# Two norms from one pass over x, and the sums of three norms set between the tiles of a projection, in a fused two-block kernel

## The chip, the cores and the metric

The kernel runs on one core of a Trainium2 chip. The metric is the time that the device takes for one run, in microseconds (us), as the median of several runs; the lower it is, the better. The core has a matrix engine (TensorE, PE in the rows, with its weight loads as PEld), a vector engine (VectorE, DVE), an engine for activation functions (ScalarE, ACT), a general engine (GpSimd, POOL), and queues that issue DMAs (SyncE's, SP, and GpSimd's). Each engine executes its instructions in the order written; they wait for each other at semaphores.

## The reference, cut to what matters

512 tokens of width 1024 go through a first block (a state-space mixer, a gated FFN with a short convolution, shared keys and values, stick-breaking attention, a second FFN), and through a second one (softmax attention over 256 context tokens and the 512 tokens, then a Hyena layer). What the change touches:

```python
# end of the first block
x = x + conv_ffn(rms_norm(x, norm_ffn[1]), ...)
x = rms_norm(x, norm_final)
# second block, i = 0: softmax attention over context and tokens
h_lat = rms_norm_2(x, norm_w[0]) * (1 + scale) + shift
h_ctx = rms_norm_2(ctx, norm_w[0]) * (1 + scale_c) + shift_c
x = x + gate * attention(h_lat, h_ctx) @ w_out
# i = 1: Hyena
h = rms_norm_2(x, norm_w[1]) * (1 + scale) + shift
x = x + gate * hyena(h) @ w_out
return rms_norm_2(x, final_norm_w)
```

with rms_norm(x, g) = x / sqrt(mean(x^2) + eps) * g, in fp32.

## The kernel before, in words

Activations lie with the width on the partitions: x is eight tiles (k = 0 to 7) of 128 x 512. Large projections run as three matmuls in a 22-bit format instead of one in fp32: weights and inputs are split into a high and a low part. A weight tile of 128 output columns arrives in panels (`raw`, four buffers); ScalarE makes the high part of a panel (`split_hi`, line 1231), GpSimd the low one (`split_lo`, line 1677), and TensorE multiplies hi*hi, lo*hi and hi*lo. The parts have two buffers: `split_hi(n)` waits until TensorE has read panel n - 2. `lin_split` takes one panel for a tile (so `split_hi` of tile t + 2 waits for tile t), the FFN's second projection (`down`) three panels for a tile. After each tile VectorE adds it to x (`add_x`), which raises `x_ready`. `beside(m)` names work that a projection puts behind tile m, `mid(t)` work in the middle of tile t.

A wide norm goes like this: ScalarE squares the eight k tiles (`row` or `norm`), into four buffers, so that square k + 4 waits for the sum of k (`sq_used`). TensorE sums each over the partitions with four matmuls of 32 columns against ones (`sums`, or `norm` at line 508). ScalarE takes the root (line 1210), VectorE the reciprocal (line 1825), TensorE spreads it over all partitions (`spread`, line 527), and VectorE scales (`norm`, lines 1840 and 1843) and adds the shift (lines 1846 and 1849). `keep_clock(n)` puts n matmuls of the unit matrix, 256 columns, in TensorE's order (line 469).

The order of each engine is written out by hand. In the first FFN the norm `kv` already has its squares and sums beside the tiles of `down0`. Behind `down1` the order of TensorE is: norm "final" (sums, spread), norm "nw0" of its result (sums, spread), sums of the context, then "qa" (line 544) from the modulated tokens, with the context's spread behind qa's second tile; then keys and values of both, from one buffer HA that holds context and tokens. The context comes by a DMA in GpSimd's queue, issued when all of down1's tiles are done (line 1750). The norm "nw1" stands behind "wo2", the projection of the softmax attention (its sums before the Hyena filters, line 1052, its spread between them), and "final2" behind "wo3", at the end of the kernel. In wo2 two small matmuls of the filters' hidden layer stand behind tiles 1 and 4 (`hidden`, line 1026).

Of the kernel before, what the change touches and what calls it, by code (L numbers as in the profile page):

```python
# [27 lines left out]
P = 128  # L28
D = 1024
# [41 lines left out]
def build(nc, A, out):  # L71
    ctx = ExitStack()
    with ctx:
# [38 lines left out]
        def col(n, i=0, r=P):  # L112
# [13 lines left out]
            "rn_ready",  # L126
# [316 lines left out]
        R_RELEASE = {"final": ("h_ready", 16), "nw0": ("h_ready", 24), "ctx": ("h_ready", 32),  # L443
                     "final2": ("out_done", 8)}
        WIDE_NORMS = ("mix0", "ffn0", "kv", "ffn1", "final", "nw0", "ctx", "nw1", "final2")

        def sq_of(name, k):

            return bigv(P1 + k * L, L) if name in ("mix0", "ffn0", "ffn1") else sq[:, (k % 4) * L:(k % 4 + 1) * L]

        def rows_of(name):

            i, n = WIDE_NORMS.index(name), norm_src(name)[1]
            return rms[0:n // 4, (i % 2) * P:(i % 2 + 1) * P]
# [5 lines left out]
        def _(pe):  # L460
# [10 lines left out]
            def sums(name, ks):  # L471

                o = take(pe, ("norm", name)) if ks[0] == 0 else ps(("norm", name))
                for k in ks:
# [6 lines left out]
                    if name == "kv" and k < KT - 1:  # L481
                        i.then_inc(S["sq_used"], 1)
# [15 lines left out]
            def norm(name):  # L498

                src, n, m, _ = norm_src(name)  # L500
                keep_clock(3 if name == "nw0" else 0)
                o = take(pe, ("norm", name))
                for k in range(len(src)):
# [9 lines left out]
                    if k < len(src) - 1:  # L513
                        i.then_inc(S["sq_used"], 1)
                fills(i, ("norm", name))
                if name in WIDE_NORMS and name not in ("mix0", "ctx", "nw1"):
                    spread(name)
# [190 lines left out]
            def ffn(l):  # L708
# [6 lines left out]
                for m in range(KT):  # L715
# [20 lines left out]
                    if l == 0 and m == 4:  # L736
                        sums("kv", range(4))
# [122 lines left out]
            norm("final")  # L860


            norm("nw0")
            norm("ctx")
            nh[0] += 8
            lat = lambda k: HA[:, k, LC:LA]
            lin("qa", A["in_q"], 2, lat, wait=h_wait, beside=lambda m: spread("ctx") if m == 1 else None)
            enter_halves([full(("down1", 7))])
            nh[0] += 8
            pe.wait_ge(S["h_ready"], nh[0] + 8)  # L870
            nh[0] += 8
            s, wp = panel(pe, A["in_kv"][0][:, :], KT)
            for seg, (a, b) in enumerate(((0, LC), (LC, LA))):
                key = ("ka", seg)
                o = take(pe, key)
                for k in range(KT):
                    i = pe.matmul(o[:, 0:b - a], wp[:, k, 0:P], HA[:, k, a:b], start=k == 0, stop=k == KT - 1)
                fills(i, key)
            for t2 in range(2):
                key = ("va", t2)  # L880
                o = take(pe, key)
                for t_ in range(3):
                    for k in range(KT):
                        t0 = (3 * t2 + t_) * P
                        i = pe.matmul(o[:, t_ * P:(t_ + 1) * P], HA[:, k, t0:t0 + P], wp[:, k, P:2 * P],
# [8 lines left out]
            for seg, (a, b) in enumerate(((0, LC), (LC, LA))):  # L894
                for what, c0, c1, r0 in (("ckv", 0, P, 0), ("kpe", P, 160, 64)):
                    key = (what, seg)
                    o = take(pe, key)
                    for k in range(KT):
                        i = pe.matmul(o[r0:r0 + c1 - c0, 0:b - a], wp[:, k, c0:c1], HA[:, k, a:b], start=k == 0,
# [119 lines left out]
            def hidden(m):  # L1019
                if m not in HID_BESIDE:  # L1020
# [6 lines left out]

            enter_halves([full(("s", 39))])
            lin_split(lambda t: ("wo2", t), A["attn_w_out"], 8, lambda k: pe.wait_ge(S["g_hi"], k + 1),
                      lambda k: pe.wait_ge(S["g_lo"], k + 1), beside=hidden, x_base=32, h=H_PARTS["wo2"])  # L1030
# [3 lines left out]
            norm("nw1")  # L1034
# [86 lines left out]
            def convolve(t):  # L1121
# [11 lines left out]
                if t in BACK_AT:  # L1133
# [8 lines left out]
                      lambda k: pe.wait_ge(S["z_lo"], k + 1), x_base=40, h=H_PARTS["wo3"])  # L1142
            norm("final2")
# [31 lines left out]
        def _(act):  # L1175
# [38 lines left out]
            eps = small[:, 639:640]  # L1214

# [26 lines left out]
            def row(name, k):  # L1242
                x_wait(k)
                gained(name, k)
                if name == "kv" and k >= 4:
                    act.wait_ge(S["sq_used"], n_used[0] + k - 3)
                act.activation(sq_of(name, k), X[:, k, :], ACT.Square).then_inc(S["sq_ready"], 1)

            def root(name):
                act.preload_act_table_set("sqrt_and_others")  # L1250
                act.wait_ge(*full(("norm", name)))
                frees(act.activation(rows_of(name), ps(("norm", name))[:, 0:P], ACT.Sqrt, bias=eps, scale=1.0 / D),
                      ("norm", name))
                n_x[0] += 8
                n_used[0] += 7 * (name == "kv")
# [84 lines left out]
            def ffn(l):  # L1340
# [1375 lines left out]
```

## Time and profile before

| what | value |
|---|---|
| time, median of 3 runs | 2172.17 us (2170.03 to 2172.68) |
| profiled execution: span from its first to its last instruction | 2169.1 us |
| its own time, beside the span | not given apart; the median lies 3.07 us over the span |
| TensorE busy | 2086.0 us (96%) |
| VectorE busy | 1365.7 us (63%) |
| ScalarE busy | 815.8 us (38%) |
| GpSimd busy | 774.9 us (36%) |
| DMA | 201.85 MB moved, 93 GB/s on the mean |

The profile comes from one execution. Where an engine is busy nearly all the time, what counts is where it stands still and what it is made to execute; of the others, only the pieces that lie between two pieces of TensorE.

### The profile page before, as it was taken

The numbers are of one execution on the slowest core, as the hardware profiler recorded it, in microseconds if no ns is written. First come the engines' busy times: TensorE is split into PE (matmuls) and PEld (weight loads), VectorE is DVE, ScalarE is ACT, GpSimd is POOL, SyncE is SP. The second block draws the span as 40 slices with busy tenths as digits, with TensorE's granted clock in tenths as the row PEclk, the third lists the DMA queues.
The fourth block names the chain that finished last, engine by engine and source line by source line (L and its number), as shares of the span: only waits on it lengthen the run. The fifth ranks groups of instructions, "written<-read, shape, count | busy, mean of one in ns | idle before, by whom it ended". The sixth has DMA issues, their size and how long they took to land.

```text
span 2169.1 us, 28247 instructions
## 1 busy us (share of the span) xinstructions
PE 2086.0 (96%) x11100; PEld 1608.4 (74%) x11100; DVE 1365.7 (63%) x2342; ACT 815.8 (38%) x1185; POOL 774.9 (36%) x462
## 2 busy tenths in 40 slices
PE   7949999999999999999999999999999999999998
PEld 6847778888878877788888875564877646777786
DVE  8563399995656478578884124257776674477752
ACT  3414333333234378333333132244664342322222
POOL 6614456555445521344444430122000322321232
PEclk9979999999999999999999999998999999999999
DMA  5032344443335421244443331012001313222221
GB/s 189 2 45 88 97 137 145 146 136 110 118 123 136 121 57 28 70 135 146 145 140 96 94 128 71 29 47 63 2 15 38 125 78 131 90 80 78 107 72 65
DMA packets 57892, 201.85 MB, mean 93 GB/s; under 512 B 10521, under 2 KB 11721, under 8 KB 54207
## 3 DMA queue, kind: packets, MB, share of 16 engines
q1 hardware_dynamic: 40464, 156.92, 22.7%
q0 software_dynamic: 13568, 41.94, 6.3%
q10 hardware_dynamic: 3728, 1.18, 0.3%
q8 instruction: 89, 1.46, 0.3%
q14 instruction: 43, 0.35, 0.1%
HBM read 179.04 MB, written 10.49 MB: 87 GB/s over the span
## 4 chain that ended last, share of the span: by engine, by line
PE 86%; DVE 8%; ACT 3%; issue 1%; POOL 1%; DMA 1%; SPq 0%; DVEq 0%; ACTq 0%; POOLq 0%
PE psum L675 15%; PE psum L682 15%; PE psum L676 15%; PE psum L725 3%; PE psum L726 3%; PE psum L727 3%; PE psum L1114 3%; PE psum L1072 3%; PE psum L1099 2%; PE psum L1000 2%; PE psum L978 2%; PE psum L968 2%; PE psum L564 2%; PE psum L544 1%; PE psum L1052 1%
## 5 line engine op out<-in xcount | busy, mean ns | idle before, releaser
L1677 POOL TENSOR_TENSOR w_lo<-raw,w_hi 128x1024 fp32r<-128x1024 f32 (+1 forms) x224 | 562.1, 2510 | 826.5 <-ACT w_hi L1231 826.3
L1231 ACT ACTIVATE w_hi<-raw 128x1024 fp32r<-128x1024 f32 (+1 forms) x224 | 233.9, 1045 | 835.8 <-PE psum L682 643.5
L675 PE MATMUL psum<-h_hi,w_hi 128*128 128x512 f32 x800 | 319.1, 399 | 1.6 <-ACT h_hi L1325 1.0
L676 PE MATMUL psum<-h_hi,w_lo 128*128 128x512 f32 x800 | 311.7, 390 | 0.0
L682 PE MATMUL psum<-h_lo,w_hi 128*128 128x512 f32 x800 | 198.0, 389 | 0.0
L675 PE MATMUL psum<-f_lo,w_hi 128*128 128x512 f32 x480 | 189.6, 395 | 2.3 <-POOL w_lo L1677 2.2
L676 PE MATMUL psum<-f_lo,w_lo 128*128 128x512 f32 x480 | 187.3, 390 | 0.0
L675 PEld LDWEIGHTS psum<-h_hi,w_hi 128*128 128x128 f32 x800 | 150.3, 188 | 38.5 <-ACT h_hi L1325 3.3
L676 PEld LDWEIGHTS psum<-h_hi,w_lo 128*128 128x128 f32 x800 | 150.3, 188 | 32.1 <-issue 2.2
L682 PEld LDWEIGHTS psum<-h_lo,w_hi 128*128 128x128 f32 x800 | 150.0, 188 | 31.3 <-issue 0.2
L1221 ACT ACTIVATE big<-psum 128x384 f32<-128x384 f32 (+6 forms) x182 | 90.0, 533 | 165.0 <-PE psum L978 47.6
L725 PE MATMUL psum<-f_hi,w_hi 128*128 128x512 f32 x352 | 138.0, 392 | 0.4
L726 PE MATMUL psum<-f_hi,w_lo 128*128 128x512 f32 x352 | 137.2, 390 | 0.0
L682 PE MATMUL psum<-f_lo,w_hi 128*128 128x512 f32 x496 | 124.1, 390 | 0.0
L682 PEld LDWEIGHTS psum<-f_lo,w_hi 128*128 128x128 f32 x496 | 92.8, 188 | 19.5 <-issue 0.4
L675 PEld LDWEIGHTS psum<-f_lo,w_hi 128*128 128x128 f32 x480 | 90.1, 188 | 22.6 <-issue 2.4
L676 PEld LDWEIGHTS psum<-f_lo,w_lo 128*128 128x128 f32 x480 | 90.2, 188 | 18.2
L2144 DVE SCALAR_TENSOR_TENSOR ffn_buf<-scr,cols,ffn_buf 128x511 f32<-128x511 f32 x44 | 71.8, 1632 | 43.5 <-ACT ffn_buf L1360 43.4
L727 PE MATMUL psum<-f_lo,w_hi 128*128 128x512 f32 x224 | 87.2, 389 | 0.0
L725 PEld LDWEIGHTS psum<-f_hi,w_hi 128*128 128x128 f32 x352 | 66.1, 188 | 15.9 <-POOL w_lo L1677 1.6
L726 PEld LDWEIGHTS psum<-f_hi,w_lo 128*128 128x128 f32 x352 | 66.1, 188 | 13.2
L1828 DVE RECIPROCAL rms<-rms 128x512 f32<-128x512 f32 (+1 forms) x9 | 27.0, 2998 | 74.6 <-ACT rms L1210 74.6
(439 smaller groups left out, 4133.4 us busy)
## 6 DMA issues: line engine op xcount, KB each, us to landing
raw<-in_ffn_w_up SPq DMA_DIRECT2D x88, 512.0 KB, 3.6
raw<-in_ffn_w_down SPq DMA_DIRECT2D x32, 512.0 KB, 3.5
raw<-in_hy_in SPq DMA_DIRECT2D x32, 512.0 KB, 5.7
ffn_buf<-in_ada_w POOLq DMA_DIRECT2D x28, 512.0 KB, 5.1
sq<-in_ada_w POOLq DMA_DIRECT2D x20, 512.0 KB, 5.0
raw<-in_ssm_w_glu SPq DMA_DIRECT2D x16, 512.0 KB, 3.6
spec<-big SPq DMA_DIRECT2D x8, 1024.0 KB, 3.8
big<-spec SPq DMA_DIRECT2D x8, 1024.0 KB, 4.9
```

The costliest lines, as they stand in the source:

```text
L675: pe.matmul(o, hi[:, k, :], h_of(k), start=k == 0, stop=False)
L676: pe.matmul(o, lo[:, k, :], h_of(k), start=False, stop=False)
L682: i = pe.matmul(o, hi[:, k, :], l_of(k), start=False, stop=k == KT - 1)
L725: pe.matmul(o, hi[:, k, :], FHI[:, kk, :], start=kk == 0, stop=False)
L726: pe.matmul(o, lo[:, k, :], FHI[:, kk, :], start=False, stop=False)
L727: i = pe.matmul(o, hi[:, k, :], flo(l, kk), start=False, stop=kk == FT - 1)
L1072: i = pe.matmul(o, tab[:, 2 * par + t, f * P:(f + 1) * P], FE[u % 2][:, a // 2, 2 * par + t, :], start=t == 0, stop=t == 1)
L1114: i = pe.matmul(o[:, par * 256:par * 256 + 256], YW[:, f, 2 * q + par, c * P:(c + 1) * P], tab[:, f, par * 256:par * 256 + 256], start=f = ...
L1221: frees(act.activation(dst, ps(key) if src is None else src, func, **kw), key)
L1231: act.activation(w_parts(n)[0], raw[:, (n % 4) * HALF:(n % 4) * HALF + w], ACT.Copy).then_inc(S["w_hi"], 1)
L1677: pool.tensor_tensor(lo, raw[:, (n % 4) * HALF:(n % 4) * HALF + w], hi.bitcast(F32), ALU.subtract) \
L2144: step(STT(g[:, 1:L], z[:, 0:L - 1], col(f"conv{l}", FT + m), g[:, 1:L], ALU.mult, ALU.add))
```

## The change

Six edits, in three places.

1. The norms "final" and "nw0". With r the inverse root mean square of x, the norm of the final norm's result is r * x * w over the root of mean((r x w)^2) + eps; with both sides multiplied by 1 / r, the second root is taken of mean(w^2 x^2) + eps * (mean(x^2) + eps), that is of mean((w^2 + eps) x^2) + eps^2. So both norms need one pass over x: ScalarE squares each k twice, once as it is and once scaled by the root of w^2 + eps (a column, `sum_weight`), and TensorE sums both into two halves of one bank. This happens beside the tiles of down1, one k per tile, as in down0; the modulated tokens are scaled from x itself before x is normed. "final" is spread behind qa's second tile.
2. The context's squares, sums, root, spread and scaling move into down1 (behind its tiles 1 to 4), in place in XC; its DMA is issued in down1. Keys and values read the context from XC instead of HA (`tokens`).
3. The tokens' shift goes from VectorE to ScalarE (`Identity` with a bias column).
4. The square-root table is loaded at the start of down1, and no longer between the norms; for nw1 and final2 the load goes from before the squares to behind them (`root`).
5. The squares and sums of "nw1" stand beside wo2's tiles and those of "final2" beside wo3's: ScalarE squares row t - 1 behind `split_hi` of panel t + 2; TensorE sums rows 0 to 3 behind tile 4 and row m - 1 behind tile m from 5 on.
6. `keep_clock` before a spread has six matmuls instead of three, for nw0 and final2; the three before nw0's sums go.

```diff
+        SPACED = ("kv", "nw0", "nw1", "final2")
...
+                    if name == "nw0":
+                        for j in range(4):
+                            i = pe.matmul(o[32 * j:32 * j + 32, P:2 * P], mat("ones")[:, 0:32],
+                                          weighted_sq(k)[:, j * P:(j + 1) * P], start=False, stop=k == KT - 1,
+                                          skip_group_check=True)
...
-                keep_clock(3 if name in ("final", "nw0", "final2") else 0)
+                keep_clock(6 if name in ("nw0", "final2") else 0)
...
-                    if l == 0 and m == 4:
-                        sums("kv", range(4))
+                    if m == 4:
+                        sums("nw0" if l else "kv", range(4))
+                    if l:
+                        if m == 2:
+                            norm("ctx")
+                        if m == 3:
+                            spread("ctx")
+                        if m >= 5:
+                            sums("nw0", (m - 1,))
...
-            norm("final")
-            norm("nw0")
-            norm("ctx")
+            sums("nw0", (KT - 1,))
+            spread("nw0")
...
-            lin("qa", A["in_q"], 2, lat, wait=h_wait, beside=lambda m: spread("ctx") if m == 1 else None)
+            lin("qa", A["in_q"], 2, lat, wait=h_wait, beside=lambda m: spread("final") if m == 1 else None)
...
+            def beside_wo2(m):
+                hidden(m)
+                if m == 4:
+                    sums("nw1", range(4))
+                if m >= 5:
+                    sums("nw1", (m - 1,))
...
-            norm("nw1")
+            sums("nw1", (KT - 1,))
...
-                      lambda k: pe.wait_ge(S["z_lo"], k + 1), x_base=40, h=H_PARTS["wo3"])
-            norm("final2")
+                      lambda k: pe.wait_ge(S["z_lo"], k + 1), x_base=40, h=H_PARTS["wo3"],
+                      beside=lambda m: sums("final2", range(4) if m == 4 else (m - 1,)) if m >= 4 else None)
+            sums("final2", (KT - 1,))
+            spread("final2")
... ScalarE: the squares, the root, the end of down1's gates
+                if name in SPACED and k >= 4:
                     act.wait_ge(S["sq_used"], n_used[0] + k - 3)
-                act.activation(sq_of(name, k), X[:, k, :], ACT.Square).then_inc(S["sq_ready"], 1)
+                i = act.activation(sq_of(name, k), X[:, k, :], ACT.Square)
+                if name == "nw0":
+                    i = act.activation(weighted_sq(k), X[:, k, :], ACT.Square, scale=sum_weight(k))
+                i.then_inc(S["sq_ready"], 1)
...
             def root(name):
-                act.preload_act_table_set("sqrt_and_others")
+                if name != "nw0":
+                    act.preload_act_table_set("sqrt_and_others")
...
                 gate_hi(FT - 1)
+                if l:
+                    act.preload_act_table_set("sqrt_and_others")
                 for n in range(n0 + 2 * FT + 2, n0 + HALVES):
                     split_hi(n)
                     m = (n - n0 - 2 * FT) // 3
-                    if l == 0 and (n - n0 - 2 * FT) % 3 == 2 and m:
-                        row("kv", m - 1)
+                    if (n - n0 - 2 * FT) % 3 == 2 and m:
+                        if l and m == 1:
+                            context_squares()
+                            ...
+                        row("nw0" if l else "kv", m - 1)
+                        if l and m == 3:
+                            context_root()
... ScalarE: wo2 (wo3 alike, with "final2")
                 split_hi(HALVES_AT["wo2"] + t + 2)
                 if t == 3:
                     hidden(0)
+                if t:
+                    row("nw1", t - 1)
             hidden(1)
             act.wait_ge(S["hid_ready"], 2)
-            norm("nw1", ready=x_wait)
+            for k in range(5, KT):
+                row("nw1", k)
+            root("nw1")
... GpSimd
+                if n == 2 * FT + 2:
+                    pool.wait_ge(*full(("up1", 2 * FT - 1)))
+                    pool.dma_start(XC[:, :, :], A["ctx"][:, :, :]).then_inc(S["ctx_in"], 16)
... VectorE
-            norm("final", lambda k: col("final", k), lambda k: X[:, k, :])
-            norm("nw0", ...)
-            norm("ctx", ...)
+            dve.wait_ge(*full(("rb", "nw0")))
+            for k in range(KT):
+                STT(HA[:, k, LC:LA], X[:, k, :], adac(0, 1, k), ps(("rb", "nw0")), ALU.mult, ALU.mult) \
+                    .then_inc(S["lat_scaled"], 1)
+            ...
+            dve.wait_ge(*full(("rb", "final")))
+            for k in range(KT):
+                STT(X[:, k, :], X[:, k, :], col("final", k), ps(("rb", "final")), ALU.mult, ALU.mult) \
+                    .then_inc(S["x_normed"], 1)
```

## Rows read from the trace of the kernel before

**Rows 1.** The page: busy time of each engine, share of the span, instructions.
```profile
PE 2086.0 (96%) x11100; PEld 1608.4 (74%) x11100; DVE 1365.7 (63%) x2342; ACT 815.8 (38%) x1185; POOL 774.9 (36%) x462
```

**Rows 2.** The chain of waits, 1286 to 1334: start us, length us, what.
```profile
1286.52 0.84 PE psum L508 x24
...
1304.51 14.88 PE psum L544 x32
...
1320.02 13.93 PE psum L544 x32
```

**Rows 3.** The timeline of the gap: start us, length us, engine, line, operation, count [idle before].
```profile
1287.28 0.69 DVE L2031 TENSOR_TENSOR X<-scr,X 128x512 f32<-128x512 f32 x1
...
1289.24 0.16 PEld L508 LDWEIGHTS psum<-sq,mats 128*32 128x32 f32 x8 [0.36 <-ACT sq L1198]
...
1291.24 1.13 PE L527 MATMUL psum<-rms,mats 128*128 128x128 f32 x8
...
1292.41 5.36 DVE L1840 SCALAR_TENSOR_TENSOR X<-X,cols,psum 128x512 f32<-128x512 f32 x8 [1.31 <-PE psum L527]
1293.25 5.18 ACT L1198 ACTIVATE sq<-X 128x512 f32<-128x512 f32 x8 [1.84 <-DVE X L1840]
...
1294.02 0.93 PE L508 MATMUL psum<-sq,mats 128*32 128x128 f32 x16 [0.36 <-ACT sq L1198]
```

**Rows 4.** The timeline of wo2, tile 6's start, and of its end.
```profile
1707.71 0.39 PE L675 MATMUL psum<-h_hi,f_hi 128*128 128x512 f32 x1
...
1707.97 1.06 ACT L1231 ACTIVATE f_hi<-raw 128x1024 fp32r<-128x1024 f32 x1 [5.62 <-PE psum L682]
...
1718.79 0.75 DVE L2035 SCALAR_TENSOR_TENSOR X<-psum,ada,X 128x512 f32<-128x512 f32 x1 [3.60 <-PE psum L682]
1719.23 2.19 ACT L1198 ACTIVATE sq<-X 128x512 f32<-128x512 f32 x4 [6.17 <-PE psum L508]
...
1721.84 0.70 PE L1052 MATMUL psum<-big 65*128 65x512 f32 x1
```

**Rows 5.** The timeline of the end of wo3.
```profile
2154.82 0.75 DVE L2035 SCALAR_TENSOR_TENSOR X<-psum,ada,X 128x512 f32<-128x512 f32 x1 [4.69 <-PE psum L682]
...
2158.00 0.37 ACT L1210 ACTIVATE rms<-psum,small 128x128 f32<-128x128 f32 x1 [0.55 <-PE psum L508]
...
2159.50 1.13 PE L527 MATMUL psum<-rms,mats 128*128 128x128 f32 x8
```

**Rows 6.** ScalarE's timeline at both ends of down1; TensorE's waits, 1160 to 1290.
```profile
1174.42 0.83 ACT L1231 ACTIVATE w_hi<-raw 128x768 fp32r<-128x768 f32 x1
...
1277.96 1.28 ACT L1190 ACT_TABLE_LOAD   x1
1279.26 2.19 ACT L1198 ACTIVATE sq<-X 128x512 f32<-128x512 f32 x4
...
PEld psum L725 <- POOL w_lo L1677: 0.5, 1, 0.5
```

**Rows 7.** TensorE's timeline: one group of sums in ffn1, four in down0.
```profile
925.73 0.39 PE L676 MATMUL psum<-h_hi,w_lo 128*128 128x512 f32 x1
926.04 0.42 PE L478 MATMUL psum<-big,mats 128*32 128x128 f32 x8
926.40 2.12 PE L682 MATMUL psum<-h_lo,w_hi 128*128 128x512 f32 x8
...
585.31 1.08 PE L478 MATMUL psum<-sq,mats 128*32 128x128 f32 x32
```

**Rows 8.** ScalarE's timeline and groups of context squares; the context's DMA (KB, us to landing).
```profile
1192.62 1.06 ACT L1231 ACTIVATE w_hi<-raw 128x1024 fp32r<-128x1024 f32 x1 [4.59 <-PE psum L727]
...
L1198 ACT ACTIVATE sq<-Hb 128x256 f32<-128x256 f32 x8 | 2.7, 405 | 0.5 <-PE psum L508 0.5
...
Hb<-in_ctx POOLq DMA_DIRECT2D x1, 1024.0 KB, 5.2
```

**Rows 9.** Busy time by window: us, PE, PEld, DVE, ACT, POOL, granted clock, DMA share, GB/s.
```profile
1297.00:1301.00 4.00, 3.76 (x29) 2.20 (x30) 1.72 (x3) 3.14 (x6) 0.00 (x0) 0.57 0.01 2
```

More of the change, by code:

```diff
@@ L876, in _ @@
                 for k in range(KT):
-                    i = pe.matmul(o[:, 0:b - a], wp[:, k, 0:P], HA[:, k, a:b], start=k == 0, stop=k == KT - 1)
+                    i = pe.matmul(o[:, 0:b - a], wp[:, k, 0:P], tokens(k, a, b), start=k == 0, stop=k == KT - 1)
                 fills(i, key)
@@ L1214, in _ @@
             eps = small[:, 639:640]
+            eps_squared = small[:, 638:639]
             def x_wait(k):
@@ L1441, in _ @@
             ffn(1)
-            norm("final", ready=x_wait)
-            n_x[0] += 8
-            norm("nw0", ready=lambda k: act.wait_ge(S["h_ready"], 8 + k + 1))
-            act.wait_ge(S["ctx_in"], 16)
-            norm("ctx")
+            row("nw0", 7)
+            root("nw0")
+            for k in range(KT):
+                act.wait_ge(S["lat_scaled"], k + 1)
+                act.activation(HA[:, k, LC:LA], HA[:, k, LC:LA], ACT.Identity, bias=ada[:, 2 * k:2 * k + 1]) \
+                    .then_inc(S["h_ready"], 1)
             def lat_parts(ks):
                 for k in ks:
-                    act.wait_ge(S["h_ready"], 16 + k + 1)
+                    act.wait_ge(S["h_ready"], 8 + k + 1)
                     act.activation(LAT_HI[k], HA[:, k, LC:LA], ACT.Copy).then_inc(S["lat_hi"], 1)
@@ L1618, in _ @@
                 split_hi(HALVES_AT["wo3"] + t + 2)
-            norm("final2", ready=x_wait)
+                if t:
+                    row("final2", t - 1)
+            for k in range(5, KT):
+                row("final2", k)
+            root("final2")
         @block.gpsimd
@@ L1745, in _ @@
                     ada_load(ADA_ISSUE[1][n])
+                if n == 2 * FT + 2:
+                    pool.wait_ge(*full(("up1", 2 * FT - 1)))
+                    pool.dma_start(XC[:, :, :], A["ctx"][:, :, :]).then_inc(S["ctx_in"], 16)
             pool.wait_ge(S["x_ready"], 32)
-            for m in range(8):
-                pool.wait_ge(*full(("down1", m)))
-            pool.dma_start(XC[:, :, :], A["ctx"][:, :, :]).then_inc(S["ctx_in"], 16)
+            pool.wait_ge(*full(("norm", "nw0")))
             pool.dma_start(ROPE[:, :, :], A["rope"][:, :, :]).then_inc(S["rope_in"], 16)
@@ L2089, in ada_finish @@
                     own()
+                fv = cols[:, COLS["final"]:COLS["final"] + 8]
+                weights_ = ada[:, 49:65:2]
+                step(TT(ada[:, 16:32:2], ada[:, 16:32:2], fv, ALU.mult))
+                step(TT(weights_, fv, fv, ALU.mult))
+                own()
+                step(TS(weights_, weights_, EPS, None, ALU.add))
+                own()
             def norm_split(name, gain, shift, ks, r):
@@ L2166, in finish @@
                         ada_finish()
+                    if m == 3:
+                        dve.wait_ge(*free(("norm", "ctx")))
+                        dve.reciprocal(rows_of("ctx"), rows_of("ctx")).then_inc(S["rn_ready"], 1)
+                    if m == 4:
+                        dve.wait_ge(*full(("rb", "ctx")))
+                        for k in range(KT):
+                            step(STT(XC[:, k, :], XC[:, k, :], adac(0, 1, k, 1), ps(("rb", "ctx"))[:, 0:LC], ALU.mult,
+                                     ALU.mult))
+                            own()
+                            TS(XC[:, k, :], XC[:, k, :], adac(0, 0, k, 1), None, ALU.add).then_inc(S["ctx_ready"], 1)
                 add_x(f"down{l}", beside=finish if l else beside, factor=8 + 16 * l, then=None if l else "kv")
@@ L2241, in _ @@
             ffn(1)
-            norm("final", lambda k: col("final", k), lambda k: X[:, k, :])
-            dve.wait_ge(S["h_ready"], 16)
-            norm("nw0", lambda k: adac(0, 1, k), lambda k: HA[:, k, LC:LA], shift=lambda k: adac(0, 0, k))
-            norm("ctx", lambda k: adac(0, 1, k, 1), lambda k: HA[:, k, 0:LC], shift=lambda k: adac(0, 0, k, 1))
+            dve.wait_ge(S["lat_root"], 1)
+            dve.reciprocal(rows_of("nw0"), rows_of("nw0")).then_inc(S["rn_ready"], 1)
+            dve.wait_ge(*full(("rb", "nw0")))
+            for k in range(KT):
+                STT(HA[:, k, LC:LA], X[:, k, :], adac(0, 1, k), ps(("rb", "nw0")), ALU.mult, ALU.mult) \
+                    .then_inc(S["lat_scaled"], 1)
+            dve.wait_ge(*free(("norm", "nw0")))
+            dve.reciprocal(rows_of("final"), rows_of("final")).then_inc(S["rn_ready"], 1)
+            dve.wait_ge(*full(("rb", "final")))
+            for k in range(KT):
+                STT(X[:, k, :], X[:, k, :], col("final", k), ps(("rb", "final")), ALU.mult, ALU.mult) \
+                    .then_inc(S["x_normed"], 1)
             for k in range(KT):
```

72 lines of the change are left out of this document (49 added, 23 removed).

## The prediction

> **What bounds the kernel now.** First the page's busy shares: TensorE is busy 96% of the span, VectorE 63% [rows 1]. What TensorE does not wait for it must run, and any matmul put between others lengthens the program. Then the chain of waits: it runs through TensorE alone inside the projections, and leaves it at the norms. At the end of the second FFN, 17.99 us lie between the last matmul of "down1" (1286.52) and the first of "qa" (1304.51), filled with two norms one after the other and the context's sums, and the first two qa tiles take 14.88 us where the next two take 13.93: VectorE hands a k over more slowly there than TensorE's 0.87 us (13.93 / 16) [rows 2]. Then the timeline of that gap, for the delay of each hand-over [rows 3], and the same for the two other stretches that the diff touches, the end of wo2 [rows 4] and of wo3 [rows 5]. The own time: the span is 2169.1 us, the median of the three timed runs 2172.17, so I put 3.1 us around the span and add the sum to both.
>
> **1. The table load moves onto the path: +1.4 us.** Before, the load of the square-root table stands at 1277.96, 1.28 us, behind the last split of weights, and nothing waits for it. Now it stands between the last gate and the split of the third panel of down1's first tile. That split, 0.83 us at 1174.42, starts as soon as ScalarE has done the gate, goes straight to GpSimd and on to TensorE, which already waits 0.5 us for it: the only wait of the whole of down1 [rows 6]. So the load delays TensorE by its whole length and the 0.1 us by which ScalarE starts an instruction before the last has ended: 1.4. The two later loads in the gap go, but both stood beside other work.
> The Trainium skill, "ScalarE: Activation LUTs", section "What ACT_TABLE_LOAD costs", gives about 2.66 us for a switch, a drain included; here ScalarE's squares start 0.02 us behind the load's 1.28, at 1279.26, so the trace disagrees [rows 6]. By the page this term would be 2.7 and the total 1.3 us higher.
>
> **2. Sums beside down1's tiles: +6.45 us.** One group of four 32-column matmuls was already put into a dense stream: the regular matmul that would have come at 925.96 (0.23 us pitch behind 925.73) comes at 926.40, and the eight behind it take 2.12 instead of 1.98 us: 0.58 us for one group. Four groups (32 rows) take 1.08 instead of 0.42 to 0.43 us, so a further group adds 0.21 [rows 7]. The context has eight groups (0.58 + 7 x 0.21 = 2.05), its spread two matmuls, half of the 1.13 us of four [rows 3], plus refill: 0.75. The new norm sums two sets: k 0 to 3 behind tile 4 are eight groups, 2.05; k 4 and k 5 two groups each, 0.79 twice; k 6, behind the last tile, hides under VectorE's addition. No wait here: ScalarE squares row m-1 behind the third panel of tile m, a panel before that tile ends. In tile 1 it has 4.59 us idle before the next split (1192.62) for eight context squares (2.7), a small root (some 0.3) and two squares (1.2), 4.2 in all; if it overran, the next split would be late by the excess. The context's DMA moves forward in GpSimd's queue, past the splits of 21 panels; it is issued behind the split of that third panel, near 1179, and lands 5.2 us later by the row of its old place, 4 us before the squares ask for it [rows 8]; rope's DMA stays behind the splits, and SP's queue is not passed. VectorE's context scaling (eight pairs, some 0.9 us each) has a tile's 15 us (120 us of down1 over eight). All that: nothing.
>
> **3. The gap: -9.1 us, and -0.95 +0.45 behind it.** X is complete at 1287.97 as now. Two squares (0.52 + 0.62) end at 1289.2, as the last one does now, so the matmuls start at 1289.24; with one group more (0.36 + 0.21) they end at 1289.8. Now six clock-keeping matmuls of 256 columns stand in front of the spread instead of three; by 0.87 us for 512 columns they take 6 x 0.43 = 2.6, to 1292.4. The other way, over root and reciprocal, takes 2.00 us from the sums' start to the spread, 2.21 then, and is ready at 1291.45: the longer row of fillers costs 0.95 and is what is late next. Spread to scaling +1.17, scaling to ScalarE +0.84, ScalarE's shift to TensorE +0.77, and 0.2 for the column operands that square and shift now read: qa starts at 1295.4, 9.1 before 1304.5 [rows 3]. VectorE's pace is then 0.66 per k (5.36 / 8), ScalarE's the same, both under TensorE's 0.87, so the 0.95 us of the first tiles go too. The spread inside qa has four matmuls for two, 1.13 us for half of it and some refill: +0.45. The final norm's scaling (5.4 us) and the low parts (about 5 us) end by 1321 on VectorE, before the four qa tiles do, and only "cq", later still, asks for the low parts. **Stage: 1.4 + 6.45 - 9.1 - 0.5 = -1.75.**
>
> **4. wo2 (norm nw1): +3.1 us.** Here a tile is one panel. ScalarE squares row t-1 only after split t+2, and that split waits for tile t itself: it starts 0.26 us after the matmuls of the next tile (1707.97 against 1707.71) [rows 4]. But TensorE asks for row 4 right behind tile 5. So behind tile 5 it waits 0.26 + 0.97 (the split, 1.06, less the overlap) + 0.62 + 0.07 = 1.92, then the group 0.36, and refill 0.1: +2.4. Behind tile 4 the hidden layer's matmul (512 columns, 0.87) and three ready groups (0.8) cover nearly all of that wait: the four groups' 1.2 and 0.1 of waiting, +1.3. Tile 6: +0.6. At the end X is complete at 1719.54; now ScalarE squares four there (1719.23, 2.19 us), then one, ending at 1720.2, and the filters start at 1720.6 instead of 1721.84: -1.2 [rows 4]; the table load now behind the squares lies beside the filters. While TensorE stands, nobody else is relieved: the splits are ahead already.
>
> **5. wo3 (norm final2): +5.3 us.** The same order, and no hidden layer as cover: behind tile 4 and behind tile 5 TensorE waits for a split that began when the tile ended and for the square behind it: +2.4 each; tile 6 +0.6. At the end X is complete at 2155.57, the square ends at 2156.2, the sums at 2156.7. The table load (1.28, now behind the squares instead of before them) puts the root at 2157.5 instead of 2158.00, and the spread, 1.5 behind it, at 2159.0; the six fillers, 2.6 from 2156.7, let it start at 2159.3 to 2159.5, against 2159.50: -0.1 [rows 5]. What the earlier sums win goes to the fillers.
>
> **Sum:** -1.75 + 3.1 + 5.3 = +6.65; span 2175.8, time 2172.2 + 6.6 = 2178.8.
>
> **Bounds.** A group between tiles was seen only in two forms [rows 7]; from below it is the bare 0.36 us from its start to the next matmul, which takes 0.22 off at eleven places: +4.2. From above, add an overrun in tile 1 (0.5) and a slow-clock stretch (1.7): +8.9. I take 0.58, as the nearest row is the same group in the same kind of stream. The likeliest case's own range is 2176.4 to 2181.
>
> **Rivals.**
> (a) *The waits in wo2 and wo3 don't arise*: the squares would come before the splits end up waiting. Then behind tile 5 of wo2 and tiles 4 and 5 of wo3 only the groups are paid (0.6, 1.2, 0.6), 4.8 us less: +1.8, 2174.0. For: ScalarE is idle 5.62 us before the split at 1707.97. Against: it executes in order, and this split is released by TensorE's own tile [rows 4]. 0.16.
> (b) *The clock falls under qa.* Between 1297 and 1301 the granted clock was 0.57 on the mean, so partly at its lower level (1.2 instead of 2.4 GHz), after TensorE had worked in pieces since 1286.5 [rows 9]; mostly fillers and waits lie in it. If the stretch came as late after 1286.5 in the new kernel, it would lie on dense qa matmuls and take 4 x (1 - 0.57) = 1.7 us: 2180.5. The Trainium skill, "TensorE: Matmul & The Clock Gate", section "HAM oscillation — how this bites in real kernels", says that waits between bursts bring the half clock back; by this rule, the trace agrees for the longer gap. Against: the gap is half as long. 0.14.
> (c) *Faster: inserted groups are nearly free.* They use 32 columns, and if they slipped in between the 128-column matmuls, 11.25 us of groups in my sum (6.45, 2.4, 2.4) would vanish, while some 0.6 more of waiting would show: -4.0, 2168.2. It turns faster when the groups cost less than 41% of my price. Against: 926.40 for 925.96. 0.09.
> (d) *The gap doesn't shrink as said*, as the spread waits for something else: each us lost there is one us more; at 3 us, 2181.8. 0.06.
> The forecast keeps 0.55. A change under 0.2%, 4.3 us, is about what a measurement can't tell from none. "Within" takes (a) and a small part (0.07) of the forecast's low side: 0.23; faster 0.09, all of (c), whose time lies just at that bound; slower 0.68. Range 2171.5 to 2182: from the low side of (a) to (d).
>
> **What would show it.** After: the table load between gate and split near 1174.5, and the third panel's matmul near 1178.6; down1 6 to 8 us longer; 8.9 us instead of 18 between its end and qa; six fillers (12 rows) ending when the spread starts; TensorE idle about 1.8 us behind tile 5 of wo2 and 1.2 to 1.8 behind tiles 4 and 5 of wo3, released by ScalarE's squares; the last scaling starting as long after wo3's end as now. The forecast is wrong if these waits are missing, or if the groups show a start-to-start cost under 0.3 us.

## The result and the profile after

The changed kernel takes 2181.11 us (median of 11 runs, 2177.61 to 2198.36), the kernel before beside it 2170.28 (11 runs, 2167.17 to 2172.68): ratio 1.0054, 95% interval 1.0039 to 1.0068. I had forecast 2178.8, slower, in 2171.5 to 2182. A second set gave 2181.79 (8 runs) against 2171.57, ratio 1.0072 [1.0043, 1.0102].

The times of the changed kernel fall into two groups, which those of before (up to 2175.8 in 109 executions) never did: 4 of the 19 lie at 2197.8 to 2198.9, some 17 us above the rest. I call these the tail. (Two more lie between, at 2184.6 and 2186.4.) The first profile caught one of the 4 (span 2196.6), so I read a second execution, of 2178.9 us and a span of 2177.1, for everything but that tail. Its page (busy time, share of the span, instructions) answers to [rows 1]: TensorE has as many instructions and 1.8 us less busy time, in a span 8.0 longer.

```profile
PE 2084.2 (96%) x11100; PEld 1610.2 (74%) x11100; DVE 1374.1 (63%) x2338; ACT 818.4 (38%) x1192; POOL 772.3 (35%) x462
```

**The gap behind down1.** The chain of waits of the second execution (start, length, what), for [rows 2]:

```profile
1297.23 0.63 ACT sq L1283
1297.86 0.62 ACT ffn_buf L1285
...
1298.53 0.43 PE psum L495 x8
1298.95 0.22 PE psum L500 x8
1299.17 2.79 PE psum L486 x12
1301.96 0.91 PE psum L546 x8
...
1302.89 0.76 DVE big L2340
...
1303.67 0.73 ACT big L1511
...
1304.54 13.97 PE psum L563 x32
1318.51 0.89 PE psum L546 x8
```

The last matmul of down1 ends at 1295.76. The order is the one forecast: X complete, two squares, one pair of groups (L495, L500), six clock-keeping matmuls (12 rows of L486), which end just where the spread (L546) starts, VectorE's scaling, ScalarE's shift, qa. The gap is 8.78 us instead of 17.99, and qa's first tiles take 13.97 instead of 14.88. Root and reciprocal are not in the chain: the fillers (the clock-keeping matmuls) are what is late. In the first profile they run partly at the lower clock and take 3.89 us, and the gap is 10.31 us.

**The end of up1 and down1's first tiles.** ScalarE's timeline (start, length, engine, line, operation, count [idle before]), for [rows 6, 8]:

```profile
1175.76 1.28 ACT L1429 ACT_TABLE_LOAD   x1
1177.05 0.85 ACT L1266 ACTIVATE w_hi<-raw 128x768 fp32r<-128x768 f32 x1
...
1190.55 2.56 ACT L1305 ACTIVATE Hb<-Hb 128x256 f32<-128x256 f32 x8
...
1195.24 1.06 ACT L1266 ACTIVATE w_hi<-raw 128x1024 fp32r<-128x1024 f32 x1 [0.76 <-PE psum L746]
```

The table load stands between gate and split and ends where the split begins. The context's squares and two of the norm's end 0.76 us before the next split: nothing overran.

**wo2 and wo3.** The chain through tile 5 of wo2 (and the first filter, L1084), through tile 4 of wo3, and at wo3's end, for [rows 4, 5]:

```profile
1705.63 1.83 PE psum L701 x8
1707.48 0.76 DVE X L2111
...
1708.50 0.62 ACT big L1283
1709.16 0.43 PE psum L495 x8
...
1715.05 1.81 PE psum L701 x8
...
1724.82 1.06 PE psum L1084 x2
...
2139.57 1.83 PE psum L701 x8
2141.47 1.06 ACT w_hi L1266
2142.53 0.53 ACT sq L1283
2143.10 0.43 PE psum L495 x8
...
2165.00 2.79 PE psum L486 x12
...
2168.72 0.75 DVE X L1915
```

In wo3 the path leaves TensorE for the split (L1266) and the square behind it, and comes back for one group of sums. TensorE's waits in both stages, as the view of the timeline puts them:

```profile
1709.16 0.43 PE L495 MATMUL psum<-big,mats 128*32 128x128 f32 x8 [1.72 <-ACT big L1283]
...
2143.10 0.43 PE L495 MATMUL psum<-sq,mats 128*32 128x128 f32 x8 [0.93 <-ACT sq L1283]
```

Behind tile 5 of wo3 it is 1.7 again. In wo2 the chain goes over VectorE's addition to X, which ends 0.26 us before the square starts. ScalarE's timeline shows what the square stood behind, the split that the end of tile 5 released:

```profile
1707.54 1.06 ACT L1266 ACTIVATE f_hi<-raw 128x1024 fp32r<-128x1024 f32 x1 [6.26 <-PE psum L701]
1708.50 0.61 ACT L1283 ACTIVATE big<-X 128x512 f32<-128x512 f32 x1
```

By stages, from the chains of the profiled execution of before and of the second execution of the changed kernel:

| stage, from and to | before | after | difference | forecast |
|---|---|---|---|---|
| start of up1's last gate to down1's last matmul | 112.61 | 120.63 | +8.0 | +7.85 |
| gap to qa | 17.99 | 8.78 | -9.2 | -9.1 |
| first two qa tiles, and the spread behind them | 15.52 | 14.86 | -0.7 | -0.5 |
| wo2: hidden layer's matmul to the first filter | 20.71 | 25.22 | +4.5 | +3.1 |
| wo3: first matmul to the norm's first scaling | 46.53 | 51.69 | +5.2 | +5.3 |
| sum | | | +7.8 | +6.65 |

The last 0.2 us of the 8.0 are 1.2 by which the changed kernel already came late to the end of up1, and -1.0 between qa and wo2, where stretches at a lower clock lie elsewhere (below).

**The clock behind wo2's waits.** Busy time by window (us; PE, PEld, DVE, ACT, POOL; granted clock; DMA share, GB/s). First the second execution, behind tile 5 of wo2, then the long one, from tile 5 of wo2 on:

```profile
1708.00:1712.00 4.00, 2.84 (x15) 2.12 (x16) 3.97 (x4) 2.26 (x4) 2.39 (x1) 0.75 0.00 0
1712.00:1716.00 4.00, 4.00 (x16) 3.22 (x15) 0.89 (x2) 0.00 (x0) 0.00 (x0) 0.82 0.91 340
```

```profile
1712.00:1716.00 4.00, 4.00 (x15) 3.17 (x12) 3.34 (x3) 0.71 (x2) 1.51 (x1) 0.57 0.23 77
...
1724.00:1728.00 4.00, 2.85 (x24) 1.57 (x24) 0.75 (x1) 1.81 (x2) 0.57 (x1) 1.00 0.32 61
1728.00:1732.00 4.00, 4.00 (x7) 1.58 (x6) 1.50 (x2) 1.10 (x3) 0.00 (x0) 0.67 0.88 360
1732.00:1736.00 4.00, 4.00 (x6) 1.69 (x5) 1.59 (x3) 1.26 (x2) 0.00 (x0) 0.50 0.25 104
...
1756.00:1760.00 4.00, 4.00 (x6) 1.69 (x5) 2.30 (x4) 1.26 (x2) 1.18 (x2) 0.50 0.00 0
```

In both, a stretch of some 4 us, partly at the lower level (1.2 instead of 2.4 GHz), follows the wait behind tile 5, on dense matmuls: 1.6 to 1.7 us. In the long one the clock falls again just behind the end of wo2 and stays at 0.50 under the fully busy filters until 1763: some 34 us at half speed, the 17 us of the tail.

### The profile page after: what moved, and what is told of

It reads as the page before. It is cut to its first block, busy times and chain, and to the rows that moved or that the text cites. A ratio compares the mean times of both kernels' runs of the same rounds, so it can differ in the third digit from the quotient of the medians.

```text
span 2196.6 us, 28241 instructions
## 1 busy us (share of the span) xinstructions
PE 2104.9 (96%) x11100; PEld 1618.6 (74%) x11100; DVE 1367.8 (62%) x2338; ACT 818.5 (37%) x1192; POOL 781.8 (36%) x462
## 4 chain that ended last, share of the span: by engine, by line
PE 84%; DVE 8%; ACT 3%; POOL 2%; issue 1%; DMA 1%; SPq 0%; DVEq 0%; ACTq 0%; POOLq 0%
PE psum L694 15%; PE psum L701 15%; PE psum L695 15%; PE psum L744 3%; PE psum L745 3%; PE psum L746 3%; PE psum L1104 3%; PE psum L1146 3%; PE psum L1131 2%; PE psum L1025 2%; PE psum L1003 2%; PE psum L993 2%; PE psum L1084 2%; PE psum L583 2%; POOL w_lo L1751 1%
## 5 line engine op out<-in xcount | busy, mean ns | idle before, releaser
L1751 POOL TENSOR_TENSOR w_lo<-raw,w_hi 128x1024 fp32r<-128x1024 f32 (+1 forms) x224 | 570.1, 2545 | 829.4 <-ACT w_hi L1266 829.2
L1266 ACT ACTIVATE w_hi<-raw 128x1024 fp32r<-128x1024 f32 (+1 forms) x224 | 233.8, 1045 | 834.8 <-PE psum L701 643.8
```

Source lines behind the costliest of these rows:

```text
L1266: act.activation(w_parts(n)[0], raw[:, (n % 4) * HALF:(n % 4) * HALF + w], ACT.Copy).then_inc(S["w_hi"], 1)
L1751: pool.tensor_tensor(lo, raw[:, (n % 4) * HALF:(n % 4) * HALF + w], hi.bitcast(F32), ALU.subtract) \
```

## The experiments

Ratios are to the kernel before, run beside each; the bracket is the 95% interval.

**1. The changed kernel again** (no edit).

> The changed kernel once more, unchanged, since its first profile is of a run of 2198 us where the median is 2181. Theory (waits and groups): a run near 2181 has no stretch at the lower clock in the filters behind wo2 (that one had TensorE at 0.50 from 1732 to 1760, which alone is 14 us or more), but does have about 3.3 us at the lower clock under the fillers behind down1 (+1.4 over the forecast) and a shorter one behind tile 5 of wo2 (+1.7): span near 2178, ratio 1.005. Rival (the excess over the forecast is spread over the whole span): no such stretches, all stages some 0.2% longer.

2181.79, 1.0072 [1.0043, 1.0102]. The loss repeats. Its profile is the second execution above. Of the two stretches at the lower clock that I expected, the one behind tile 5 of wo2 is there; the one under the fillers is not (2.79 us for the six).

**2. Squares ahead of splits** in wo2 and wo3:

```
-                split_hi(HALVES_AT["wo2"] + t + 2)
-                if t == 3:
-                    hidden(0)
                 if t:
                     row("nw1", t - 1)
+                split_hi(HALVES_AT["wo2"] + t + 2)
+                if t == 3:
+                    hidden(0)
... wo3 alike
```

> In wo2 and wo3 ScalarE squares row t-1 ahead of the split of panel t+2 instead of behind it; nothing else. Theory: TensorE's waits behind tile 5 of wo2 and tiles 4 and 5 of wo3 go (4.8 us by the forecast's terms: 1.8, 1.2, 1.8), and with the first also the stretch at the lower clock behind it (up to 1.7): 2181 less 4.8 to 6.5, so 2174.5 to 2176.2. Rival (the inserted matmuls themselves cost, the waits would be there in another form): 2180 to 2181.

2173.74 (12 runs), 1.0035 [1.0013, 1.0056]. Eight executions lie at 2170.3 to 2174.6, four at 2189.3 to 2191.2. The medians lie 7.4 and 8.1 us under those of the changed kernel, more than the 4.8 to 6.5 that I expected, but they hold different shares of the tail. Outside the tail it is 2173.5 here against 2178.7 for the five executions of the changed kernel in the same set (5.2 us), or 2180.6 for its 15 of both sets (7.1 us). The chain through wo2's tiles:

```profile
1698.57 1.00 PE psum L1051 x2
...
1704.43 1.81 PE psum L701 x8
...
1710.45 1.81 PE psum L701 x8
```

Tile 5 to tile 6 takes 6.02 us (1704.43 to 1710.45) instead of 9.42 (1705.63 to 1715.05): the wait of 1.7 is gone, and the lower clock behind it with it, 1.6 more. In wo3 tile 4 gives 7.83 to 6.67 and tile 5 7.83 to 6.03. That is 3.4 + 3.0, and 0.2 behind tile 4 of wo2: 6.6 us in the trace, of which some 4.8 are the waits, as forecast, and 1.6 the clock. The rival (no gain) falls. The waits are ScalarE's order and no more.

**3. The down1 part alone**: only "kv" and "nw0" in SPACED; norm("nw1") and norm("final2") as before, three fillers in wo3:

```
-SPACED = ("kv", "nw0", "nw1", "final2")
+SPACED = ("kv", "nw0")
...
-            sums("nw1", (KT - 1,))
+            norm("nw1")
```

> Only the part at down1 (two norms from one pass, context early, shift by ScalarE, table early, six fillers for nw0); nw1 and final2 as in the kernel before, with three fillers for final2. Theory: what is left is -1.75 by the forecast plus 1.4 for the lower clock under the fillers: within 1.5 us of the kernel before, ratio 0.999 to 1.001. Rival (the loss lies in the down1 stage, for instance by its inserted sums): 4 us or more over before, ratio 1.002 to 1.005.

2170.72 (11 runs, up to 2173.68), 0.9997 [0.9989, 1.0006]. The loss lies wholly in wo2 and wo3, and so does the tail: it comes in none of these 11 executions, nor in the 44 of experiments 5, 6, 7 and 11, whose wo2 and wo3 are as before too. That the part gains nothing measurable fits its -1.75: in this execution the six fillers ran at a lower clock and took 4.47 us instead of 2.79, and the gap was 10.5 us.

**4. The table load a panel later**:

```
-                if l:
-                    act.preload_act_table_set("sqrt_and_others")
                 for n in range(n0 + 2 * FT + 2, n0 + HALVES):
                     split_hi(n)
+                    if l and n == n0 + 2 * FT + 3:
+                        act.preload_act_table_set("sqrt_and_others")
```

> The changed kernel with the load of the square-root table two splits later in down1, behind the fourth panel instead of ahead of the third. Theory: the load stood on the path with its 1.28 us and 0.1 of lost overlap: 1.4 us less than the changed kernel, near 2179.7. A switch of 2.66 us would give 2.7 less, near 2178.4. Rival (TensorE would wait there anyway): no difference, 2181.

2179.28 (10 runs, four of them at 2194.9 to 2197.7), 1.0061 [1.0035, 1.0087]. The tail blurs the time (outside it the median is 2177.7 for six executions, 1.0 under the changed kernel's five in the same set); the chain does not. ScalarE's last gate starts at 1174.60, the first matmul of the third panel starts at 1177.91, 3.31 us on; in the changed kernel it is 1175.13 and 1179.84, 4.71 us. So 1.40 on the path, what I had for it:

```profile
1175.11 0.84 ACT w_hi L1266
...
1176.02 1.85 POOL w_lo L1751
...
1177.91 0.50 PE psum L744
```

The Trainium skill, "ScalarE: Activation LUTs", section "What ACT_TABLE_LOAD costs", has about 2.66 us for a switch; this trace doesn't agree, with 1.40 for load and all that hung on it.

**5. and 6. The down1 part with the later load, with six and with three fillers**:

```
-                keep_clock({"nw0": 6, "final2": 3}.get(name, 0))
+                keep_clock(3 if name in ("nw0", "final2") else 0)
```

> The down1 part of the change alone (wo2 and wo3 with their norms behind the last tile, as before), and ScalarE's load of the square-root table put behind the split of the fourth panel of down1's first tile instead of ahead of the third. Theory (the load delays TensorE by its 1.28 us and 0.1 of start, and has cover one panel later; the other table-later kernel moved the first matmul of the third panel from 4.71 to 3.31 us behind the end of ScalarE's gate): 1.4 us under the down1 part alone (2170.7 beside 2170.3 to 2171.6 of the kernel before), so 2169.3, ratio to before 0.999. Rival (what is saved at the start of down1 is given back to a stretch at the lower clock elsewhere): 2170.7, no change. The same run tests the other side of the tail that only kernels with spaced sums in wo2 and wo3 have shown (executions 17 us above the median): theory none here, as in the down1 part alone.

> The same kernel with three clock-keeping matmuls instead of six ahead of the spread in the gap behind down1 (wo3 has three as before). Theory: in the changed kernel's trace the sums of k 7 start at 1298.53, the six take 2.79 us and the spread starts at 1301.96; root and reciprocal are ready some 2.2 us behind the start of the sums, 1300.7; three would end at 1300.6. So the spread starts 1.2 us earlier: 2168.1. In executions where the clock is at its lower level under the fillers (4.47 us for the six in the trace of the down1 part alone) it gains up to 2.0. Rival: the three that go were what kept the clock; the stretch at the lower clock moves onto qa's dense matmuls and takes 1.7 us there: 2169.8 or above, and qa's first two tiles take more than 13.97 us.

The edit shown is that from six to three. Six: 2169.61, 0.9995 [0.9986, 1.0004], no tail. Beside the 0.9997 of experiment 3, which came from another set, that shows no gain where I expected 1.4 us; intervals of some 2 us to either side can't show one. The 1.40 rests on the chain. Three: 2167.33 (11 runs), 0.9985 [0.9974, 0.9996], 2.3 under six in the same set, the first version whose interval lies under the kernel before. Its gap:

```profile
1295.98 0.43 PE psum L493 x8
...
1296.62 2.53 PE psum L484 x6
1299.15 1.53 PE psum L544 x8
...
1302.35 13.97 PE psum L561 x32
```

Sums to qa take 6.37 us instead of 7.70 in the kernel with six (1297.78 to 1305.48), both partly at the lower clock, and qa keeps its 13.97. Here the three fillers beyond what root and reciprocal take are pure cost.

**7. No fillers there** (`keep_clock(3 if name == "final2" else 0)`).

> The down1 part with the later table load (2167.3 with three clock-keeping matmuls ahead of the gap's spread, 2169.6 with six), now with none there. Theory (they set the spread's time only while they outlast root and reciprocal): root and reciprocal take some 2.2 us from the start of the sums to the spread, the three end 2.0 to 3.2 us behind it, so 0 to 1 us is left to gain, while TensorE then stands for 1.6 us more in the gap: if that brings the lower clock to qa's first tiles it costs 1.7 or more. I take both: 2166.8 to 2168.5, no clear change to three. Rival (they are pure cost): 2166.3. Second rival (they keep the clock, for good): 2169 and above, with a granted clock under 1 behind 1304 in the trace.

2169.56, 0.9996 [0.9987, 1.0005], outside the 2166.8 to 2168.5 that I expected. The medians lie 2.2 over that with three; by the ratios, since the sets differ, it is 2.4 over experiment 6 and 1.3 over its repetition (11), and the intervals overlap. So the times alone don't settle it. The trace (one execution) shows the second rival:

```profile
1296.10 0.64 PE psum L493 x8
...
1297.63 0.96 DVE rms L2327
...
1298.73 2.06 PE psum L544 x8
...
1302.46 15.93 PE psum L561 x32
```

The spread now starts behind the reciprocal, 2.63 us after the sums' start instead of 3.17, but the spread itself takes 2.06 and qa's first two tiles 15.93, since TensorE's clock, down in the gap, is still down when qa begins:

```profile
1296.00:1300.00 4.00, 2.34 (x22) 1.91 (x23) 0.95 (x1) 0.67 (x3) 0.57 (x1) 0.52 0.21 35
1300.00:1304.00 4.00, 2.31 (x6) 1.32 (x6) 3.18 (x5) 2.40 (x4) 0.00 (x0) 0.50 0.54 227
1304.00:1308.00 4.00, 4.00 (x8) 1.65 (x7) 3.03 (x5) 4.00 (x8) 0.00 (x0) 0.70 0.00 0
```

With three, the last two of these windows have 0.96 and 1.00. This is rival (b) of the prediction, met in another kernel, at 1.96 us (15.93 less 13.97) for my 1.7.

**8. and 9. The waits of wo2 filled**: in the changed kernel behind tile 5 and at the end of wo2, and in that of experiment 2 at the end alone:

```
+                if m == 5:
+                    keep_clock(4)
                 if m >= 5:
                     sums("nw1", (m - 1,))
...
+            keep_clock(3)
             sums("nw1", (KT - 1,))
```

> The changed kernel with TensorE's waits in wo2 filled: four clock-keeping matmuls (256 columns, 0.46 us each, 1.86) ahead of the sums of k 4 behind tile 5, where it waits 1.73 us, and three (1.4) ahead of the sums of k 7 behind tile 7, where it waits 1.15 to 1.4 us. Theory (idle time of TensorE in this stage is what brings the lower clock: behind tile 5 the granted clock was 0.57 over 4 us, and in some executions 0.50 over 34 us under the filters): the sums come no earlier, so the waits' own time stays (+0.1 us); the low stretch behind tile 5 goes (-1.7) and with it the executions near 2197: 2179.5 beside 2181.1 to 2181.8, and no execution above 2186. Rival (the stretches come whatever TensorE does just before them): times as the changed kernel's, 3 of 10 executions near 2197.

> The kernel with the squares ahead of the splits (2173.7; 4 of its 12 executions at 2189 to 2191), and three clock-keeping matmuls ahead of the sums of k 7 behind wo2's last tile. In that kernel TensorE has no wait behind tile 5, and still has the tail. Theory (the idle time at the end of wo2, just ahead of the filters, is what brings the 17 us): median 2173.5, no execution above 2180. Rival (something else in the spaced stages brings it): a third of the executions stay near 2190.

Experiment 8: 2179.34 (5 runs, up to 2181.07), 1.0036 [1.0022, 1.0051]. Tile 5 to tile 6 now takes 7.82 us (1705.47 to 1713.29) for 9.42: the sums come no earlier, the lower clock goes, 1.6 us. All three profiled executions with the wait unfilled (the two of the changed kernel and that of experiment 4) have exactly the 9.42. Experiment 9: 2172.48 (11 runs, up to 2174.93), 1.0006 [0.9997, 1.0015]. The tail had come in 12 of 41 executions of experiments 1, 2 and 4 and of the first set; with the waits filled it came in none of 16, in experiments 10 and 12 in none of 22 more. In experiment 9 three matmuls at the end of wo2 are all that differs from experiment 2, with 4 of 12. TensorE there stood 1.15 us in experiment 2 (first fence), and not at all in 9 (second):

```profile
1718.22 0.43 PE L495 MATMUL psum<-big,mats 128*32 128x128 f32 x8
1719.80 0.43 PE L495 MATMUL psum<-big,mats 128*32 128x128 f32 x8 [1.15 <-ACT big L1283]
```

```profile
1719.88 1.56 PE L486 MATMUL psum<-mats 128*128 128x256 f32 x6
1721.38 0.43 PE L495 MATMUL psum<-big,mats 128*32 128x128 f32 x8
```

The kernel before has all eight groups of sums in that place, and its matmuls wait at most 0.4 us between them. So the spaced sums, by taking work out of the wait, laid it bare. Two things weaken the case for the tail. If the three matmuls did nothing, the four long executions among these 23 would by chance all fall to experiment 2 in some 6% of cases (an estimate from the counts). And one rival is not tested: experiments 1 to 4 ran on one chip, and those with the end of wo2 filled on two others, on which, as far as is on record (the chip of the first set is not), no kernel with the unfilled wait ran. The lower clock behind tile 5 does not have this doubt, as experiment 2, on the same chip as 1, took it away too.

**10. to 12. Everything mended, and does spacing pay in wo2 and wo3 at all?** The whole change with squares first, the end of wo2 filled, three fillers and the later load; then once more beside the kernel of experiment 6.

> The whole change, spaced sums in wo2 and wo3 too, with all that the runs mended: squares ahead of the splits, three clock-keeping matmuls ahead of the last sums of wo2, three instead of six ahead of the spreads, the table load a panel later. Against the same kernel without the spaced sums in wo2 and wo3 (2167.3) it tells whether spacing pays there at all. Theory (each group costs 0.6 us between tiles and saves less at the end): from the traces wo2 is 1.2 us longer than before (hidden layer's matmul to the end of the filters' first part, 40.19 against 38.97), wo3 2.2 longer with six and 1.75 with three: 2170.3. Rival (spacing pays once nothing waits for it, since 24 rows of sums leave the two ends): 2166 or below.

> The down1 part alone with the later table load and three clock-keeping matmuls, unchanged, beside the next kernel in one set of runs, since their medians (ratios to before 0.9985 and 0.9992) came from two sets. Theory: 2167.3, ratio 0.9985, and 3 us under the next kernel, by the traces: its wo2 takes 40.19 us from the hidden layer's matmul to the end of the filters' first part against 38.97, its wo3 48.48 from the first matmul to the norm's first scaling against 46.55, 3.1 us together. Rival (spacing pays elsewhere what it costs here, by fewer stretches at the lower clock): the same time as the next.

> The whole change with all that was mended, unchanged, beside the kernel above. Theory: 3.1 us over it, 2170.4, ratio to before 0.9999. Rival: no difference (within 1 us), 2168.2 or below. No execution near 2190 by either, since the waits of wo2 are gone or filled.

2168.16 where I expected 2170.3, 0.9992 [0.9983, 1.0001]; then side by side 2166.85, 0.9990 [0.9981, 0.9999], without spacing there, and 2168.40, 0.9991 [0.9982, 1.0000], with it. Over 22 executions each, the medians are 2167.1 and 2168.2, the means 2167.6 and 2168.7, each with a standard error of 0.4 to 0.5: 1.2 us apart with an error of 0.6. I had expected 3.1. The traces have 1.2 us more in wo2 (40.19 for 38.97, hidden layer's matmul to the filters) and 1.9 in wo3 (48.48 for 46.55), 3.1; the medians show 1.1. So no gain from spacing there is shown, and its cost is barely clear of noise; where 2 us of it come back in the whole program I can't say. Nor is spacing at its best in wo3: with three fillers the chain at its end goes through the table load, root and reciprocal, as the load now stands behind the last square (2157.15 to 2158.43), where the kernel before has it ahead of the squares. TensorE stands 0.84 us ahead of the spread. A load placed earlier was not tried. In their traces the stretches at a lower clock outside these stages differ by more than that from one execution to the next. The best version is that of experiments 6 and 11, 2 to 3 us under the kernel before.

## Why the prediction was right, and where not

- *The number: in the range, partly by luck.* I added +6.65 to 2172.17, the median of three runs; the 11 runs beside the changed kernel have 2170.28. The change itself is +10.8 and +10.2, over the +8.9 of my upper bound. Moved down to the base of each set, my range would have ended at 2180.1 and 2181.4, just under the two medians. The direction and each of the waits were forecast; the size of the whole was not.
- *Table load, +1.4.* Right, by experiment 4: 1.40 in the chain. The times are too coarse to show it.
- *Sums beside down1's tiles, +6.45.* Right: the stage is 8.0 us longer, less 1.4 is 6.6. Of that, tile 5 of down1 with its two groups takes 15.76 us from start to start (1248.96 to 1264.72), 0.8 over the 14.99 of a tile before, the 0.58 + 0.21 of the working. Rival (c), groups nearly free, is refuted there.
- *Nothing waits in tile 1.* Right, with 0.76 us to spare.
- *Gap, -9.1.* -9.2 in the second execution. The row of fillers was named as what is late next, and is. Its 2.6 us are 2.79 at full clock; in other executions the fillers run partly at the lower clock and take up to 4.47 us (experiment 3), and there the gap gives 7.5 us (17.99 to 10.46).
- *qa, -0.95 + 0.45.* -0.9 and +0.25.
- *wo2, +3.1: the step that was too small, +4.5.* Its parts: behind tile 4 +1.15 (forecast 1.3), behind tile 5 +2.4 (2.4, from the 7.82 us of experiment 8 against 5.44 before), tile 6 +0.6 (0.6), the end -1.2 (-1.2). The remaining 1.6 is no wait but the lower clock that followed the wait behind tile 5. I had priced a slow stretch behind the gap, as rival (b), and once in the upper bound, and had not asked of the waits that I myself put into wo2 whether one would follow them. Experiments 2 and 8 show that this stretch goes when the idle time goes.
- *wo3, +5.3.* +5.2: +2.4 behind tile 4, +2.4 behind tile 5, +0.6, and -0.2 at the end (-0.1). The same kind of wait (0.93 and 1.73 us) brought no lower clock here, so such a wait alone is not enough; what else it takes is open.
- *The total.* By traces +7.8 for +6.65. By medians it is +10.8 and +10.2. The 15 executions outside the tail have a median of 2180.6, 9.8 over before, of which the profiled one, at 2178.9, is one of the faster. So some 2 us of the ordinary executions are not in its trace. Slow fillers in the gap could be most of that (10.31 for 8.78 us in the first profile), but how often they come is not shown; it stays open.
- *What no step held:* the 17 us in a fifth of the executions. No row that I had read of before pointed to it, and the median hides it: the mean of the 19 is 2184.3. What the runs suggest in its place is the 1.15 us of idle time at the end of wo2, with the doubts of experiment 9.

## What to carry to other kernels

An instruction squeezed into an in-order queue comes as late as the one ahead of it: before sums are spaced between tiles, look at what the engine that feeds them has queued in front, and put the feeder first. Work that stood in a wait was free there and costs 0.6 us a group between tiles; taking it out also lays TensorE's idle time bare, and three cheap matmuls put back can be worth more than they cost. A few fillers, just so many as the other path takes, were better than six, and by the trace better than none. Look at the spread of the times, not their median alone, and compare medians only within one set of runs: those of the unchanged kernel moved by 1.7 us from one set to the next, as much as the effects measured here.

## What the runs showed of the hardware that I had not expected

- Idle time of TensorE of 1.15 us, just ahead of dense matmuls, was followed by some 34 us at a granted clock of 0.50 while TensorE was fully busy, in both profiled executions of the tail (the changed kernel's first and that of experiment 4). The other ten of the 12 in 41 are known by their times and their mean clock, 0.978 to 0.980 for 0.985 and above. The same program had it in one execution and not in the next.
- A long stretch at 0.50 under a busy TensorE is not new, and idle time is not all that goes ahead of one. In every profiled execution, the kernel before's too, TensorE runs at 0.50 for some 10 us or more between 1479 and 1502, and it had no idle time from 1472 to where the stretch begins. In the kernel before:

```profile
1488.00:1492.00 4.00, 4.00 (x6) 0.69 (x4) 3.93 (x6) 0.00 (x0) 4.00 (x4) 0.50 0.00 0
```

- A 4 us stretch at a mean of 0.57 wanders: in the profiled execution of before it lies at 1468 (0.58), where the same four matmuls take 3.52 us for 1.96, in the changed kernel at 1372 and behind 1710; experiment 6 has neither of the first two, but one at 168 (0.50). It costs 1.6 to 1.7 us wherever it falls on dense work, as much as the down1 part was forecast to gain.
